# Projected heads written to DRAM already transposed and split, and two attentions in one loop

## What is computed

```python
proj = rmsnorm(x) @ w_in          # qa, ka, va: 8 heads x 64 each; c_q 256, c_kv 128, k_rope 32
qa, ka = rope(qa), rope(ka)       # mixer A: a masked softmax whose mask is a count per distance
o_a = dilated_attention(qa, ka, va)
qb = rmsnorm(c_q) @ w_uq          # mixer B: 8 heads x (64 plain + 32 rotary)
kv = rmsnorm(c_kv) @ w_ukv        # 8 heads x (64 key + 64 value); the rotary key is shared
o_b = dense_attention([q_nope, rope(q_rot)], [k_nope, rope(k_rope)], vb)
x = x + concat(rmsnorm(o_a), rmsnorm(o_b)) @ w_o
u = depthwise_conv3(rmsnorm(x) @ w_up) + b_conv
x = x + (silu(gate) * val) @ w_down   # 2816 hidden channels
y = rmsnorm(x)
```

## Time and profile before

| | |
|---|---|
| Median of 3 runs (lowest to highest) | 3114.44 us (3111.28 to 3118.08) |
| Profiled execution, span | 3114.5 us |
| Mean granted TensorE clock | 0.992 |
| TensorE busy | 3028.0 us (97%), 18064 matmuls and transposes |
| VectorE busy | 1899.6 us (61%) |
| ScalarE busy | 1258.5 us (40%) |
| DMA | 169.92 MB, 55 GB/s over the span |

### The profile page before, as it was taken

One profiled execution on the slowest core, in us unless ns is written; L12 is line 12 of the kernel. 1 busy time (PEld: TensorE's weight loads), 2 busy tenths in 40 slices (PEclk: granted clock), 3 DMA queues, 4 the chain that ended last, 5 costly groups with the idle time before them and its releaser, 6 DMA issues.

```text
span 3114.5 us, 49572 instructions
## 1 busy us (share of the span) xinstructions
PE 3028.0 (97%) x18064; PEld 2666.3 (86%) x18064; DVE 1899.6 (61%) x2950; ACT 1258.5 (40%) x2125; POOL 0.2 (0%) x4
## 2 busy tenths in 40 slices
PE   8999999999999999999999999999999999999998
PEld 7988988899888888888799899888998888888887
DVE  5549978885454554445555499788854544445455
ACT  5027756764322212222340277566643222222223
POOL 0000000000000000000000000000000000000000
PEclk9999999999999999999999999999999999999999
DMA  3212202103111111112231222011031111111122
GB/s 124 61 47 49 63 1 69 40 23 107 31 58 48 56 52 41 47 47 68 79 97 48 57 50 52 21 54 35 27 102 39 53 52 54 47 41 47 47 68 81
DMA packets 275607, 169.92 MB, mean 55 GB/s; under 512 B 143905, under 2 KB 260513, under 8 KB 275489
## 3 DMA queue, kind: packets, MB, share of 16 engines
q1 hardware_dynamic: 275488, 168.34, 18.4%
HBM read 124.27 MB, written 8.39 MB: 43 GB/s over the span
## 4 chain that ended last, share of the span: by engine, by line
PE 92%; issue 3%; ACT 2%; DVE 2%; DMA 1%; DVEq 0%; SPq 0%; ACTq 0%; PEldq 0%; PEld 0%
PE pair L473 73%; PE pair L600 7%; PE pair L576 4%; PE pair L578 4%; PE pair L588 2%; PE pair L648 2%; PE pair L478 1%; DMA stqb<-qb 0%; DVE x L1458 0%; DMA wst<-in_w_in 0%; ACT at_hi L803 0%; ACT junk L794 0%; DVE at_lo L1132 0%; DVEq L243 0%; ACT pr_a L889 0%
## 5 line engine op out<-in xcount | busy, mean ns | idle before, releaser
L473 PE MATMUL pair<-at_hi,wu_hi 128*128 128x512 f32 x1408 | 550.3, 391 | 5.7 <-DVE at_lo L1132 5.2
L473 PE MATMUL pair<-at_lo,wu_hi 128*128 128x512 f32 x1408 | 549.5, 390 | 0.0
L473 PE MATMUL pair<-at_hi,wu_lo 128*128 128x512 f32 x1408 | 549.3, 390 | 0.0
L473 PEld LDWEIGHTS pair<-at_hi,wu_hi 128*128 128x128 f32 x1408 | 265.1, 188 | 62.2 <-DVE at_lo L1132 5.7
L1458 DVE TENSOR_TENSOR x<-pair,x 128x1024 f32<-128x1024 f32 x176 | 215.1, 1223 | 166.9 <-PE pair L473 166.9
L473 PEld LDWEIGHTS pair<-at_hi,wu_lo 128*128 128x128 f32 x1408 | 265.1, 188 | 55.2
L473 PEld LDWEIGHTS pair<-at_lo,wu_hi 128*128 128x128 f32 x1408 | 265.1, 188 | 54.8
L473 PE MATMUL pair<-wd_hi,h_hi 128*128 128x512 f32 x704 | 274.8, 390 | 1.2 <-DVE x L1458 1.2
L473 PE MATMUL pair<-wd_hi,h_lo 128*128 128x512 f32 x704 | 274.2, 390 | 0.0
L473 PE MATMUL pair<-wd_lo,h_hi 128*128 128x512 f32 x704 | 274.2, 389 | 0.0
L1421 DVE SCALAR_TENSOR_TENSOR cv<-pair,cw,cv 128x1023 f32<-128x1023 f32 x42 | 53.9, 1284 | 312.7 <-ACT cv L1046 312.7
(11 more groups left out here) (192 smaller groups left out, 6805.6 us busy)
## 6 DMA issues: line engine op xcount, KB each, us to landing
ust<-in_w_up SPq DMA_DIRECT2D x88, 512.0 KB, 3.8
ust<-in_w_down SPq DMA_DIRECT2D x44, 512.0 KB, 4.1
wst<-in_w_in SPq DMA_DIRECT2D x15, 1024.0 KB, 5.5
xt<-in_x_seqs SPq DMA_DIRECT2D x18, 512.0 KB, 3.4
stqa<-qk SPq DMA_DIRECT2D x32, 256.0 KB, 3.5
stka<-qk SPq DMA_DIRECT2D x32, 256.0 KB, 3.6
x<-in_x_seqs SPq DMA_DIRECT2D x16, 512.0 KB, 6.5
wost<-in_w_o SPq DMA_DIRECT2D x8, 1024.0 KB, 5.3
```

The costliest lines, as they stand in the source:

```text
L473: mm = pe.matmul(dst, lhs, rhs, start=(i == 0), stop=(i == n - 1))
```

## The change

The projection of q and k is turned round: the weights are the stationary operand and the tokens the moving one, so that the product is channels x tokens, 512 tokens at a time. The host puts the weight columns in an order in which the first halves of four heads' rotary pairs fill one block of 128 rows and the second halves another. A block is rotated with tables of the same shape, its q also scaled by minus the scale, split, and written from one of six slots in SBUF to DRAM. Mixer B's low-rank projection goes the same way and moves ahead of q, k and v. V's two units become one product of 512 columns, whose rows are written out head by head as hi and lo columns. For each head the finished operands are then loaded from DRAM. Both attentions are one run of 16 heads; the staging, the rounds and `nm` are gone, and VectorE takes a row minimum of the negated scores instead of a maximum. The phases are four. The core of the diff:

```diff
@@ sizes
-EV_SEQ = (U_ALL - U_C) * NT
-ROT_SEQ = (2 + U_QK) * NT
-PHASES = 6
+B_HALF = 15
+B_BLOCKS = 2 * B_HALF
+QK_BLOCKS = 4 * U_QK
+V0 = B_BLOCKS + QK_BLOCKS
+BLOCKS = V0 + NT
+SLOTS = 6
+PHASES = 4
...
+        slot = [place(f"slot{i}", [P, 2, HALF], F32R, SLOT_AT[i]) for i in range(SLOTS)]
+        d_qa = scratch("d_qa", (2, 2, HEADS * 32, S))
+        d_ka = scratch("d_ka", (2, 2, HEADS * 32, S))
+        d_va = scratch("d_va", (HEADS * P, NT * P))
+        d_qn = scratch("d_qn", (2, HEADS * HA, S))
+        d_qr = scratch("d_qr", (2, 2, HEADS * 16, S))
...
@@ SP: the start of a sequence
-                sp.dma_start(cosa[:], cos_a).then_inc(s_inw, 16)
-                sp.dma_start(sina[:], sin_a).then_inc(s_inw, 16)
+                sp.dma_start(cos_tb[:], cos_bt).then_inc(s_inw, 16)
+                sp.dma_start(sin_tb[:], sin_bt).then_inc(s_inw, 16)
+                sp.dma_start(cos_ta[:], cos_at).then_inc(s_inw, 16)
+                sp.dma_start(sin_ta[:], sin_at).then_inc(s_inw, 16)
...
                 await_(sp, s_out, s * (16 * NT) + ONE)
+                sp.dma_start(uq_st[:], w_uq.rearrange("(k p) n -> p k n", p=P)).then_inc(s_bw, 16)
+                sp.dma_start(ukv_st[:], w_ukv).then_inc(s_bw, 16)
...
@@ SP: blocks out, operands in
+                def write_block(i, hi_to, lo_to, rows=P):
+                    for part, to, ready in ((0, hi_to, s_bhi), (1, lo_to, s_blo)):
+                        await_(sp, ready, s * BLOCKS + i + 1)
+                        sp.dma_start(to, block_slot(i)[0:rows, part, :].bitcast(F32)).then_inc(s_sl[i % SLOTS], 16)
...
+                def load_a(h):
+                    e, rows = h % 2, slice(h * 32, (h + 1) * 32)
+                    sp.dma_start(q2[e][:].bitcast(F32), d_qa[:, :, rows, :]).then_inc(s_opa[e], 16)
+                    for a in range(2):
+                        half = slice(a * HA, (a + 1) * HA)
+                        sp.dma_start(khh[e][half].bitcast(F32), d_ka[0, :, rows, :]).then_inc(s_opa[e], 16)
+                        sp.dma_start(kll[e][half].bitcast(F32), d_ka[1, :, rows, :]).then_inc(s_opa[e], 16)
...
+                for u in range(U_QK):
+                    d, g = (d_qa, d_ka)[u % 2], u // 2
+                    ch = slice(g * P, (g + 1) * P)
+                    for hf in range(2):
+                        i, tok = B_BLOCKS + 4 * u + 2 * hf, slice(hf * HALF, (hf + 1) * HALF)
+                        for r in range(2):
+                            write_block(i + r, d[0, r, ch, tok], d[1, r, ch, tok])
+                            if (u, hf, r) == (2, 0, 0):
+                                blocks_written(B_BLOCKS + 8)
+                                load_a(0)
+                                load_a(1)
+                        if (u, hf) in ((0, 0), (0, 1), (1, 0), (2, 1)):
+                            load_unit({(0, 0): 4, (0, 1): 5, (1, 0): 6, (2, 1): 7}[u, hf])
...
+                for h in range(HEADS - 2):
+                    await_(sp, s_sc, a0 * 8 + (h + 1) * 8)
+                    load_a(h + 2)
+                    await_(sp, s_pv, a0 * 4 + (h + 1) * 4)
+                    load_values(v2_a, d_va, h + 2, s_va)
...
@@ PE: low-rank blocks, q and k, v
+                def lora_block(i, hi, lo, chunks, ch, tok, stationary_weights=True):
+                    if i >= SLOTS:
+                        in_slot(i - SLOTS + 1)
...
+                    product(bank((i + 4) % SLOTS), passes).then_inc(s_blk, 1)
...
+                for u in range(U_QK):
+                    pe.wait_ge(s_wlo, s * U_ALL + U_C + u + 1)
+                    for hf in range(2):
+                        g, tok = 2 * u + hf, slice(hf * HALF, (hf + 1) * HALF)
+                        in_slot(B_BLOCKS - 4 if g == 0 else B_BLOCKS if g == 1 else B_BLOCKS + 2 * (g - 1))
+                        for r in range(2):
+                            ch = slice(r * P, (r + 1) * P)
+                            passes = []
+                            for k in range(NK):
+                                passes += [(w_hi[u][:, k, ch], at_hi[:, k, tok]), (w_hi[u][:, k, ch], at_lo[:, k, tok]),
+                                           (w_lo[u][:, k, ch], at_hi[:, k, tok])]
+                            product(pair[2 + (g + 1) % 2][:, r * HALF:(r + 1) * HALF], passes).then_inc(s_blk, 1)
+                pe.wait_ge(s_wlo, s * U_ALL + U_IN)
...
+                                   (at_lo[:, k, tok], wv_hi[:, k, :])]
+                    product(bank(t % 4), passes).then_inc(s_blk, 1)
...
@@ ScalarE
+                def slot_free(i):
+                    act.wait_ge(s_sl[i % SLOTS], s * SLOT_SEQ + (32 * (i // SLOTS) + ONE))
+
+                def block_hi(i, src, scale, rows=P):
+                    slot_free(i)
+                    act.wait_ge(s_blk, s * BLOCKS + i + 1)
+                    act.mul(block_slot(i)[0:rows, 0, :], src[0:rows, :], scale).then_inc(s_bhi, 1)
...
@@ VectorE
+                def rotary_lo(i, k, t1, t2, cos, sin, scale):
...
+                    dve.tensor_tensor(rp[0][:], t1, cos, ALU.mult)
+                    dve.tensor_tensor(rp[1][:], t2, sin, ALU.mult)
+                    dve.tensor_tensor(rp[2][:], t2, cos, ALU.mult)
+                    dve.tensor_tensor(rp[3][:], t1, sin, ALU.mult).then_inc(s_rm, 1)
+                    dve.wait_ge(s_rm, s * ROPES + k + 1)
+                    dve.tensor_tensor(rp[0][:], rp[0][:], rp[1][:], ALU.subtract).then_inc(s_rr, 1)
+                    dve.tensor_tensor(rp[2][:], rp[2][:], rp[3][:], ALU.add).then_inc(s_rr, 1)
+                    for r in range(2):
+                        block_lo(i + r, rp[2 * r], scale)
...
-                        dve.tensor_scalar(n, m, -scale, None, ALU.mult).then_inc(s_nm, 1)
...
+                        dve.tensor_tensor_reduce(sc, sc, logc[:, u0:u0 + S], 1.0, 3e38, ALU.add, ALU.min, m).then_inc(s_max, 1)
...
+                        if t == 5 and unit_o is not None:
+                            w_split(U_IN + unit_o, wost[:], wo_hi[unit_o][:], wo_lo[unit_o][:])
...
-                    if t == 3:
-                        w_split(U_IN + 1, wost[:], wo_hi[1][:], wo_lo[1][:])
```

More of the change, by code:

```diff
@@ L128, in encoder_kernel @@
[L128 to L134, removed]
@@ L135, in encoder_kernel @@
[L135 to L141 removed]
+        rp = [place(f"rp{i}", [P, HALF], F32, R_Q + 32 + 2 * i) for i in range(4)]
@@ new lines, in operands_b, with scores @@
+                def operands_b(e, h):
+                    pe.wait_ge(s_opb[e], s * (16 * (HEADS // 2 * OPS_B + 2)) + (h + 1) * (16 * OPS_B) + 32)
+                mixer_a = (passes_a, v2_a, operands_a, s_va)
+                mixer_b = (passes_b, v2_b, operands_b, s_vb)
+                def scores(mixer, e, t):
+                    q = slice(t * P, (t + 1) * P)
+                    for half in range(2):
+                        k = slice(half * 512, half * 512 + 512)
+                        mm = product(pair[t % 2][:, k], mixer[0](e, q, k))
+                    mm.then_inc(s_sc, 1)
@@ new lines, in body @@
+                def body(mixer, nxt, e, n, h, h_next):
+                    for off, t, a in BODY:
+                        if not off:
+                            step(mixer, nxt, e, n, h_next, t)
+                        elif nxt:
+                            step(nxt, nxt, 1 - e, n + 1, None, t)
+                        if a is not None and (a < 3 or nxt):
+                            osum(n, a)
+                        if off == 0:
+                            pv(mixer, e, n, h, t // 2 - 1, t % 2)
+                        elif t < 2 and nxt:
+                            pv(mixer, e, n, h, 3, t)
+                        elif t == 0:
+                            pv(mixer, e, n, h, 3, None)
+                        elif nxt:
+                            pv(nxt, 1 - e, n + 1, h_next, 0, 0)
@@ new lines, in _ @@
+                a0, b0 = s * (2 * HEADS), s * (2 * HEADS) + HEADS
+                operands_a(0, 0)
+                for t in range(2):
+                    in_slot(BLOCKS - 2 + 2 * t)
+                    scores(mixer_a, 0, t)
+                pe.wait_ge(s_pr, a0 * 8 + 1)
+                scores(mixer_a, 0, 2)
+                for t in range(3):
+                    step(mixer_a, mixer_a, 0, a0, None, t)
+                pv(mixer_a, 0, a0, 0, 0, 0)
+                with pe.Fori(0, HEADS // 2 - 1) as j:
+                    for e in range(2):
+                        body(mixer_a, mixer_a, e, j * 2 + (a0 + e), j, j + e)
@@ new lines, in step, with body @@
+                def step(n, t):
+                    for hb in range(2):
+                        act.wait_ge(s_pt, n * 16 + 2 * t + hb + 1)
+                        act.copy(pt_hi[t // 2 % 2][:, 4 * hb:4 * hb + 4, t % 2 * P:(t % 2 + 1) * P],
+                                 bank(4 + hb).rearrange("p (k n) -> p k n", k=4)).then_inc(s_pthi, 1)
+                def body(e, n, more, unit_o=None, near_end=None):
+                    for off, t, a in BODY:
+                        if off == 0 and t + 1 < NT:
```

(20 more changed lines are left out.)

898 lines of the change are left out of this document (409 added, 489 removed).

## The result

The changed kernel takes 3170.83 us (median of 4 runs, 3167.25 to 3173.0), the kernel before 3112.93 beside it: ratio 1.0177, 95% interval 1.0165 to 1.0189. It is 58 us slower. The forecast was 3128, with a range up to 3165: the sign is right, the size is not. The sign had been given a chance of 0.46, against 0.45 for faster.

A forecast was written before the change was run, and what follows sets the result against it. TensorE, busy 97% of the span, was taken as the bound. Its stages gave 3114.5 - 95 = 3019 us; narrow head loads added 110, some 3128, with a range of 3100 to 3160 for that case, 3005 to 3165 overall.

The forecast's parts named there:

- the sign: Whole kernel: slower than the kernel before, chance 0.46, against faster 0.45 and same 0.09.
- The removed rounds and merged products: Attention loops and q, k, v products: removed rounds save 37.5 us per sequence; 512-wide products take 130.7, 7.8 less.
- The seams: End of V through both attentions to the output projection: joined without the 7.40 wait, 428.5 us in all.
- The narrow loads: Head loads with 4 or 2 outermost runs use few DMA engines: 110 us more, some 3128; chance 0.55.
- The low-rank stage: Low-rank projection through six slots, paced by stores: 41 us, 13 more than now; 38 or 48 at other rates.
- The start: Start of each sequence: added tables and weights ahead of the second latent unit, +5 us in sequence 1, +3 in 2.
- Rival 1: Head loads: all sixteen engines take them, 3019 us, faster; chance 0.31.
- Rival 4: Head loads are narrow, but what SP sends behind them is not held up: 3053 us; chance 0.09.
- Rival 2: Head loads hold fewer engines and q too has only two: 31.4 us a head, 3200 us; chance 0.05.

The follow-up runs named there:

- inter: Changed kernel with scratch of A's q and k laid out row first, three wide transfers a head, B's rotary rows 16 at a time: 3023.97 us, ratio 0.9713.
- rows32: Changed kernel with every head load cut into runs of 32 rows (A: 12 transfers instead of 5), B's rotary rows 16 at a time: 3026.17 us, ratio 0.9722.
- forms: All the kernel's work left out; SP loads DRAM blocks by count of outermost runs. One 0.524 MB load: about 3 us for 128 runs, 6.5 for 4, 11 for 2.
- b_later: Changed kernel with what SP sends ahead of A's third head (B's first head, values, gain, output weights) moved behind the last A head's values: 3161.9 us, ratio 1.0156.
- fewbytes: inter with only 16 of 128 rows of the low-rank stage's q and k lo halves stored: 3027.65 us in one run, with a filling at its start.
- start: inter with the four rotary tables loaded behind the second latent weight unit, VectorE waiting for them only before it rotates: 3010.33 us, ratio 0.9666.
- pool: Changed kernel with the first two heads' loads issued by GpSimd on a queue of its own, same ten transfers: 3098.32 us, ratio 0.9945.
- q32: Changed kernel with only mixer A's q cut into runs of 32 rows, k and B's rotary rows left as they were: 3134.35 us, ratio 1.0069.
- split2: inter with the first q/k weight unit's split moved behind the low-rank second half's rotation, next unit's load behind the rotary blocks' stores: 3028.78 us, ratio 0.9729.

## Why the prediction was wrong

Lengths of the stages (us) from the traces, the prediction's own beside them. "Wide" is `inter`; the start of a sequence ends with the latent unit, and in sequence 2 it is counted from the MLP's last matmul.

| stage | predicted | changed kernel | wide |
|---|---|---|---|
| start of sequence 1, over before | +5 | +8.4 | +8.1 |
| start of sequence 2, over before | +3 | +6.5 | +6.6 |
| low-rank | 41 | 43.5, 44.3 | 43.7, 43.7 |
| q, k, v products | 130.7, narrow +37.7 | 173.5, 172.9 | 130.9, 132.4 |
| end of V to output projection | 428.5, narrow +17.5 | 453.6, 456.6 | 424.4, 422.8 |

- *The removed rounds and merged products:* right. Pairs of query tiles are 5.94 and 6.87 apart, as read in the earlier trace rows; the products without a hole take 130.86 against 130.7.
- *The seams:* right within 4 to 6 us in all (428.5 against 424.4 and 422.8): A to B goes on without a break.
- *The narrow loads:* the mechanism is right, as `rows32`, `inter` and `forms` show, and so is the sign that hung on it. **The step that failed is its price: 110 was predicted, and cutting the loads gives back 145 to 147.** Two terms of it were too small. Before V: 42.6 and 40.6 instead of 37.7 a sequence. V's weights landed 63 us behind the first of the head loads, where the sum had 58. SP's own issue was held up meanwhile (36 us for the ten loads, priced at 0.54 each); whether these 5 us come from it isn't shown. In A, 29.2 and 33.8 instead of 17.5 a sequence, of which 24.3 and 24.6 are TensorE's waits for `kll`. The third head waited 13.7 and 15.0 and not 5; the others together waited 10.6 and 9.6, less than the 12.5 that the sum had for them, with a head's load at 27.1 us instead of 26.4. `b_later` shows that the third head's wait is what SP had sent ahead of it; I had named B's first head and not added up its bytes with the two value tiles, the gain and the output weights. The rest, some 5 and 9, goes with the clock behind the waits, which I had charged at V and not in A. Mixer A in sequence 1, in the changed kernel and in `inter` (0.95 against 0.99; in sequence 2 it is 0.95 against 1.00):

```profile
297.38:514.00 216.62, 189.68 (x1338) 175.24 (x1339) 161.05 (x309) 148.55 (x281) 0.00 (x0) 0.95 0.26 85
...
254.63:441.65 187.02, 184.57 (x1340) 172.21 (x1341) 160.75 (x309) 148.73 (x281) 0.00 (x0) 0.99 0.30 99
```

- *The low-rank stage:* 2.5 and 3.3 more than 41, inside its range of 38 to 48. `fewbytes` shows that stores are only part. The clock was left out: at 0.92 the products, 27.2 us by the sum, keep TensorE busy for 32.8. How much of these 5.6 us the stage pays isn't shown.
- *The start:* some 3.5 us too little in each sequence. In sequence 1 I counted the bytes ahead of the second latent unit and missed VectorE's wait: it waits for all constants and tables ahead of its first lo half (3.28 idle until `sinb` lands, at 17.69), and that keeps TensorE 8.9 us instead of 5.4 at its first product. In sequence 2 that wait plays no part (4.7 at the first product, 4.9 before). The second unit's wait grew from 0.8 to 4.4, much as forecast, and what was left out is the clock: the granted clock is 0.55 from 1600 to 1610, where the second unit begins, and was 1.00 at that place before (1571 to 1581).

```profile
1600.00:1610.00 10.00, 6.73 (x32) 6.73 (x33) 3.98 (x4) 4.99 (x12) 0.00 (x0) 0.55 0.15 52
...
1571.00:1581.00 10.00, 9.72 (x86) 9.57 (x86) 6.54 (x13) 6.16 (x19) 0.00 (x0) 1.00 0.56 169
```

  `start` gives back 14 us in all.
- *Rival 1* was the sum without narrow loads, 3019. `inter` is 3024 with starts 3 us worse each; from the end of the latent unit to the output projection it takes 599 us a sequence, where the sum had 600.2. That is nearer than its terms are: the low-rank stage is 2.7 longer in each sequence and the attentions 4 and 6 shorter, so part of the agreement is luck. *Rival 4*, narrow loads that don't hold up what is behind them, was given 3053; `pool` comes nearest to that for the first two heads, and is 3098. *Rival 2* is out: a head's load took 27.1 us, not its 31.4.

The profiled execution, 3168.6, is 41 us above the sum of 3128: starts 7, low-rank 6, before V and in it 10, attentions 18. Taken against `inter` instead, some 36 of them are the price of the narrow loads, and the errors of all other terms nearly cancel. The sign was close to a toss by the forecast's own chances; it came out right because the mechanism that it hung on was right.

What stays open: in `q32` a head of A needed 24.5 to 25.7 us with 590 KB on engine 0, slower per byte than with 688 KB. What holds up SP's issue, and why three and one of the ten loads passed at once, isn't shown. The loss in `split2`, if it is one, goes with a slightly lower clock and was not traced further.

## What to carry to other kernels

A transfer's first dimension is a property of the kernel's layout, and it was worth 145 us here, more than the 89 that the change gains with wide loads. When a scratch in DRAM is written by one loop and read by another, lay it out so that both sides have rows outermost; the order of rows in a contraction is free. And price a slow transfer by all that is queued behind it and ahead of it on its slowest engine, not by its own landing.

## What the runs showed of the hardware

- An issue on SP isn't always 0.5 us: behind transfers on two and four engines, most issues took 2.8 to 10.9 us, and some 0.42 when each was spread over all (`rows32`).
- A *store* to 4 outermost runs is slower than a load from 4: its traffic went on for some 8.5 us for 0.524 MB, at 37 to 102 GB/s in its full windows, in `forms`, where that of the load took 6.5:

```profile
70.00:71.00 1.00, 0.00 (x0) 1.00 0.25 70
71.00:72.00 1.00, 0.00 (x0) 1.00 0.23 37
...
74.00:75.00 1.00, 0.00 (x0) 1.00 0.26 102
```

- The same head loads issued by GpSimd hold back SP's queue less: the waits before V are 9.7 and 7.5 us instead of 40.1 and 39.3. Their last transfers land 26.6 us after their issue, and up to 18 of their packets are under way at once, against 2 to 5 of SP's: they are spread wider.
